# The two mixers of the second block reordered: gate work in PSUM, a projection chunk and the glu product between the levels

## The reference, cut to what matters

```python
u, q, k, v, g_out, a_low = jnp.split(h @ w_in[layer], IN_SPLITS, axis=-1)
y_s5 = _s5_group(u, ...)      # complex linear recurrence over time, 32 groups of 64 states, then
                              # gelu(y), and y * sigmoid(y @ w_glu + b_glu)
y_gla = _gla_group(q, k, v, g_out, a_low, ...)
y = jnp.concatenate([y_s5, y_gla], axis=-1) @ w_out[layer]

# in _gla_group: b = cumsum of log_sigmoid(a_low @ w_alpha_up + b_alpha) / 16 over time;
# scores[i, j] = sum over channels of q[i] * k[j] * exp(b[i] - b[j]) for j <= i, else 0;
# o = scores @ v, normalized, times silu(g_out)
```

## Time and profile before

| | us |
|---|---|
| median of 3 runs (2665.13 to 2666.99) | 2666.32 |
| the profiled execution's own time | 2666.25 |
| its span, first to last instruction | 2664.0 |
| mixer of l = 2, from the first transposes to the end of its output product | 836.5 to 1008.2 |
| mixer of l = 3, likewise | 1281.8 to 1444.2 |

### The profile page before, as it was taken

How to read it: one execution, slowest core, us unless ns; L and a number is a source line. 1 busy time by engine, 2 the same in 40 slices (tenths; PEclk the granted TensorE clock), 3 DMA queues, 4 the chain that set the end, 5 groups by cost and what they waited for, 6 DMA issues and landing times. The chain is left out here.

```text
span 2664.0 us, 37526 instructions
## 1 busy us (share of the span) xinstructions
PE 2506.8 (94%) x14758; PEld 2056.7 (77%) x14758; DVE 1810.9 (68%) x2036; ACT 1309.1 (49%) x1336; POOL 681.6 (26%) x359
## 2 busy tenths in 40 slices
PE   6999999998999988999887799999999999999996
PEld 4876898976998757899665688878787878888884
DVE  1664775665866757755674677777777787777785
ACT  2344543444442123333021666767776767667772
POOL 0000000005900717800451123323232323323322
PEclk9999999999999988999897899999999999999997
DMA  9996854586864556955331599999999999999992
GB/s 337 291 324 217 262 198 131 174 277 200 267 208 149 190 190 206 281 194 163 107 111 66 214 367 331 366 328 350 347 347 349 348 346 344 352 337 358 329 366 96
DMA packets 434956, 693.86 MB, mean 260 GB/s; under 512 B 37690, under 2 KB 255894, under 8 KB 434838
## 3 DMA queue, kind: packets, MB, share of 16 engines
q1 hardware_dynamic: 407632, 677.17, 73.8%
q10 hardware_dynamic: 27206, 15.03, 2.1%
HBM read 691.10 MB, written 1.05 MB: 260 GB/s over the span
## 5 line engine op out<-in xcount | busy, mean ns | idle before, releaser
L1430 ACT ACTIVATE region_part<-ring 128x2048 fp32r<-128x2048 f32 x448 | 835.4, 1907 | 275.0 <-PE bank L840 190.8
L840 PE MATMUL bank<-ring_part,region_part 128*128 128x512 f32 x1648 | 649.1, 394 | 0.0
L2306 DVE TENSOR_TENSOR ring_part<-ring,region_part 128x2048 fp32r<-128x2048 f32 x270 | 640.3, 2404 | 2.5 <-ACT region_part L1430 2.5
L838 PE MATMUL bank<-region_part 128*128 128x512 f32 x1432 | 582.6, 407 | 6.2 <-DVE ring_part L2306 6.2
L839 PE MATMUL bank<-region_part 128*128 128x512 f32 x1296 | 512.1, 395 | 0.0
L1320 POOL TENSOR_TENSOR ring_part<-ring,region_part 128x2048 fp32r<-128x2048 f32 x54 | 268.6, 4982 | 554.6 <-ACT region_part L1430 554.6
L840 PEld LDWEIGHTS bank<-ring_part,region_part 128*128 128x128 f32 x1648 | 309.8, 188 | 71.4
L838 PE MATMUL bank<-xn_part,region_part 128*128 128x256 f32 x1152 | 327.1, 284 | 10.4 <-DVE hT_part L2009 9.1
L838 PEld LDWEIGHTS bank<-region_part 128*128 128x128 f32 x1432 | 269.7, 188 | 75.6 <-issue 14.6
L840 PE MATMUL bank<-hT_part,region_part 128*128 128x256 f32 x1152 | 325.2, 282 | 0.0
L839 PE MATMUL bank<-xn_part,ring_part 128*128 128x256 f32 x1152 | 325.0, 282 | 0.0
(11 more groups left out here) (309 smaller groups left out, 4014.9 us busy)
## 6 DMA issues: line engine op xcount, KB each, us to landing
ring<-in_moe_w_gate SPq DMA_DIRECT2D x126, 1024.0 KB, 5.1
ring<-in_moe_w_up SPq DMA_DIRECT2D x126, 1024.0 KB, 5.2
ring<-in_moe_w_down SPq DMA_DIRECT2D x126, 1024.0 KB, 4.9
ring<-in_w_ada SPq DMA_DIRECT2D x48, 1024.0 KB, 7.7
ring<-in_mod_w SPq DMA_DIRECT2D x48, 1024.0 KB, 6.1
ring<-in_w_in SPq DMA_DIRECT2D x44, 1024.0 KB, 5.7
ring<-in_w_up_act SPq DMA_DIRECT2D x22, 1024.0 KB, 5.5
ring<-in_w_up_lin SPq DMA_DIRECT2D x22, 1024.0 KB, 5.7
```

The costliest lines, as they stand in the source:

```text
L838: nc.tensor.matmul(o, split(a_hi), split(b_hi), start=start, stop=False, skip_group_check=True)
L840: return nc.tensor.matmul(o, split(a_hi), split(b_lo), start=False, stop=stop, skip_group_check=True)
L1430: return nc.scalar.activation(out_, in_, func, **kw).then_inc(*done(*event))
L2306: v.tensor_tensor(split(w), w, whole(hi), ALU.subtract).then_inc(*done("moe_lo", j, e))
```

## The change

- PE order: `S5_CHUNKS` is now the flat order 8, 1, 2, 3, 6, 7, 4. The first pair of units is followed by chunks 8 and 1, the second by chunk 2, `s5_out(0, 1)` and the whole of chunk 3; then come `s5_in(4, 5)`, chunk 6, `s5_out(2, 3)`, `s5_in(6, 7)`, chunk 7, `s5_out(4, 5)`, chunk 4, `s5_out(6, 7)`. The modulation chunks are spread anew (`S5_ADA`).
- The glu product, in halves, follows levels 64 and 32; modulation chunks 12 and 13 follow level 16; the two token halves of chunk 5 follow levels 8 and 4 (`between`). The load order follows.
- DVE turns unit 3 back as well as unit 7, and scans and turns both in PSUM. `c_parts` is ahead of unit 0, `gate_start` after unit 1, `gate_sums` after unit 3 with its combine and running sums in bank 7; the division by 16 becomes the scale of ACT's exponentials. `y_sum(0)` follows unit 5, `y_sum(1)` follows the products for `off`.
- `gD`, `gQ`, `gK` and `scO` lie over table rows of units 0 to 3, `scT` over `ffn_rows`. The zeroing of `gQ` and `gK` is gone, that of `scT` is ahead of POOL's first unit. `gla` waits for POOL's unit 2 in place of the zeroing.
- Levels 64, 32 and 16 are copied into `scT` by ACT, block by block (2, 4 and 8 copies), not by DVE's mask. ACT does `gelu(1)` and the copies of `off` after the second exponential, and the chunk 5 copy after the last. The levels use four banks.

```diff
-DVE_UNITS = (7,)
-S5_CHUNKS = [(8, 1), (2, 3), (4, 5), (6, 7)]
+DVE_UNITS = (3, 7)
+S5_CHUNKS = (8, 1, 2, 3, 6, 7, 4)
+S5_ADA = {8: (0,), 1: (1,), 2: (2, 3), 3: (4,), 6: (5,), 7: (6, 7), 4: (8, 9, 10, 11)}
+GLA_CHUNK = 5
+BLOCKED = 3
...
+            plan.append((("in", l, GLA_CHUNK), ("pe_tile", "in", l, GLA_CHUNK)))
...
+    gD = ec[:, 0:1024].rearrange("p (b n) -> p b n", b=2)
+    gQ = ec[:, 1024:2048].rearrange("p (b n) -> p b n", b=2)
+    gK = es[:, 0:1024].rearrange("p (b n) -> p b n", b=2)
+    scO = es[:, 1024:1536].rearrange("p (b c i) -> p b c i", b=2, c=2)
+    scT = ffn_rows[:, 0:1024].rearrange("p (b j c i) -> p b j c i", b=2, j=2, c=2)
...
+                    o = bank(("lg", l), ("gla_z", l, 1), (7,))
...
+                    outs = [[bank(("bu", l, u, r), s5_rotated(l, u) if u in DVE_UNITS else ("s5_g", l, u), (2 * (u % 2) + r,)) for r in range(2)] for u in pair]
...
+                s5_in(0, 1)
+                projection(8)
+                projection(1)
+                alpha_low()
+                s5_in(2, 3)
+                projection(2)
+                s5_out(0, 1)
+                projection(3)
+                pe.wait_ge(*until("in_out", l, 1))
+                s5_in(4, 5)
+                projection(6)
+                s5_out(2, 3)
+                s5_in(6, 7)
+                projection(7)
+                s5_out(4, 5)
+                projection(4)
                 s5_out(6, 7)
-                key = ("glu", l)
-                pe.wait_ge(*loaded(key))
-                pe.wait_ge(*until("s5_gelu", l, 1))
...
+                def glu(b):
+                    key = ("glu", l)
+                    pe.wait_ge(*loaded(key))
+                    pe.wait_ge(*until("s5_gelu", l, 1))
+                    w = chunk(key)
                     o = bank(("glu", l, b), ("s5_sig", l, b), (b,))
...
+                def late_tokens(t):
+                    key = ("in", l, GLA_CHUNK)
...
+                    if t == 0:
+                        late[0] = bank(key, ("in_out", l, GLA_CHUNK), (4,)).rearrange("p (t n) -> p t n", t=NT)
+                    for k in range(KD):
+                        m = nc.tensor.matmul(late[0][:, t, :], hT[:, k, t * P:(t + 1) * P], w[:, k, :], start=k == 0, stop=k == KD - 1)
+                    if t:
+                        m.then_inc(*done("pe_tile", *key))
+                def between(n):
+                    if n < 2:
+                        glu(n)
+                    if n == 2 and l == 2:
+                        for q in range(12, ADA_MIX):
+                            ada_sum(3, "mix", q, 0)
+                    if n in (3, 4):
+                        late_tokens(n - 3)
+                usable[0] = (2, 3, 6, 7)
...
+                o = [bank(("off", l, par), ("gla_blocks", l, "off", par)) for par in range(2)]
...
+                    o = [bank(("lv", l, n, par), ("gla_blocks" if n < BLOCKED else "lv_out", l, n, par)) for par in range(2)]
...
-                pe.wait_ge(*until("off_out", l, 1))
+                    between(n)
+                pe.wait_ge(*until("gla_blocks", l, "off", 1))
+                pe.wait_ge(*until("gla_blocks", l, BLOCKED - 1, 1))
...
+                    pool.wait_ge(*until("pe_used", "down", l - 1, 0, ffn_groups(l - 1) - 1))
+                    nc.gpsimd.memset(scT, 0.0).then_inc(*done("gla_zero", l))
                     for u in range(8):
                         if u not in DVE_UNITS:
                             rotate(l, u)
-                    pool.wait_ge(*until("s5_y", l, 1))
-                    nc.gpsimd.memset(scT, 0.0).then_inc(*done("gla_zero", l, 0))
-                    nc.gpsimd.memset(gQ, 0.0).then_inc(*done("gla_zero", l, 1))
-                    nc.gpsimd.memset(gK, 0.0).then_inc(*done("gla_zero", l, 2))
...
-                for n in (0, 8, 1, 2, 3):
...
+                for n in (0, 8, 1, 2):
+                    features_out(n)
                 act.wait_ge(*until("gla_abs", l))
                 run(gz[:, 1], gz[:, 1], ACT.Exp, "act_chain", l, "lse")
                 act.wait_ge(*done.prev())
                 run(gz[:, 1], gz[:, 1], ACT.Ln, "gla_ln", l, bias=1.0)
-                for n in (4, 5, 6, 7):
+                features_out(3)
...
+                def gelu(qq):
                     act.wait_ge(*until("s5_y", l, qq))
                     v = uT[:, 2 * qq:2 * qq + 2, :].rearrange("p c s -> p (c s)")
                     run(v, v, ACT.Gelu_apprx_tanh, "s5_gelu", l, qq)
+                def blocks(n):
+                    h = LEVELS[n]
+                    for par in range(2):
+                        p_ = tile("lv", l, n, par).rearrange("p (a i) -> p a i", a=4)
+                        o = scT[:, par].rearrange("p j c i -> p (j c) i")
+                        for r in range(0, P, 2 * h):
+                            last = r + 2 * h == P
+                            run(o[r:r + h, :, r + h:r + 2 * h], p_[r:r + h, :, r + h:r + 2 * h], ACT.Copy,
+                                *(("gla_blocks", l, n, par) if last else ("act_chain", l, "block", n, par, r)))
+                for n in (6, 7):
+                    token_out(n)
+                gelu(0)
+                token_out(4)
+                load_rows(l, "mix")
+                act.wait_ge(*until("gla_zero", l))
                 for m, half in enumerate([P] + LEVELS[:-1]):
                     act.wait_ge(*until("gla_d", l, half))
-                    run(gD[:, m % 2, :], gD[:, m % 2, :], ACT.Exp, "gla_e", l, half)
-                    if m == 0:
+                    run(gD[:, m % 2, :], gD[:, m % 2, :], ACT.Exp, "gla_e", l, half, scale=1.0 / 16)
+                    if m == 1:
+                        gelu(1)
                         for par in range(2):
                             p_ = tile("off", l, par)
-                            run(scO[:, par].rearrange("p c i -> p (c i)"), p_[:, 0:S], ACT.Copy, "off_out", l, par)
+                            run(scO[:, par].rearrange("p c i -> p (c i)"), p_[:, 0:S], ACT.Copy, "gla_blocks", l, "off", par)
+                    if 2 <= m < 2 + BLOCKED:
+                        blocks(m - 2)
+                    if m == len(LEVELS) - 1:
...
+                    z = psum[bank_of["lg", l]]
                     dve.wait_ge(*until("gla_ln", l))
-                    v.scalar_tensor_tensor(gz[:, 0], gb, 0.0, gz[:, 1], ALU.min, ALU.subtract).then_inc(*link())
-                    after()
-                    v.tensor_scalar(gz[:, 0], gz[:, 0], 1.0 / 16, None, ALU.mult).then_inc(*link())
+                    after()
+                    v.scalar_tensor_tensor(z, gb.rearrange("p c s -> p (c s)"), 0.0, gz[:, 1].rearrange("p c s -> p (c s)"), ALU.min, ALU.subtract).then_inc(*link())
                     after()
                     for c in range(2):
-                        v.tensor_tensor_scan(gb[:, c, :], ones[:, 0:1].broadcast_to([P, S]), gz[:, 0, c, :], 0.0, ALU.mult, ALU.add)\
-                            .then_inc(*link())
+                        v.tensor_tensor_scan(gb[:, c, :], ones[:, 0:1].broadcast_to([P, S]), z[:, c * S:(c + 1) * S], 0.0, ALU.mult, ALU.add)\
+                            .then_inc(*(done("gla_z", l, 1) if c else link()))
...
+                c_parts()
                 dve.wait_ge(*until("tables", l))
                 after()
...
+                    if u >= 2 and u not in DVE_UNITS:
                         dve.wait_ge(*until(*s5_rotated(l, u - 2)))
                     for r, w in ((0, im), (1, re)):
...
+                            v.tensor_tensor_scan(w[:, jj, :] if u in DVE_UNITS else g5[:, u % 2, r, jj, :], s5p[:, l - 2, 0, j:j + 1].broadcast_to([P, S]),
...
+                        h = h5[:, u % 2]
                         dve.wait_ge(*until("pe_tile", "s5o", l, u - 2))
-                        v.tensor_tensor(h[:, 0], c, gg[:, 0], ALU.mult).then_inc(*link())
-                        v.tensor_tensor(w5[:, 0], s, gg[:, 1], ALU.mult).then_inc(*link())
-                        v.tensor_tensor(h[:, 1], s, gg[:, 0], ALU.mult).then_inc(*link())
-                        v.tensor_tensor(w5[:, 1], c, gg[:, 1], ALU.mult).then_inc(*link())
+                        v.tensor_tensor(h[:, 0], c, im, ALU.mult).then_inc(*link())
+                        v.tensor_tensor(h[:, 1], s, im, ALU.mult).then_inc(*link())
                         after()
-                        v.tensor_tensor(h[:, 0], h[:, 0], w5[:, 0], ALU.subtract).then_inc(*link())
-                        v.tensor_tensor(h[:, 1], h[:, 1], w5[:, 1], ALU.add).then_inc(*done(*s5_rotated(l, u)))
-                    after()
-                    if u == 0:
-                        c_parts()
-                    if u == 2:
+                        v.tensor_tensor(im, s, re, ALU.mult).then_inc(*link())
+                        v.tensor_tensor(re, c, re, ALU.mult).then_inc(*link())
+                        after()
+                        v.tensor_tensor(h[:, 0], h[:, 0], im, ALU.subtract).then_inc(*link())
```

(36 more changed lines are left out.)

78 lines of the change are left out of this document (26 added, 52 removed).

## The result

The changed kernel takes **2637.39 us** (median of 4 runs, 2635.92 to 2644.56), the kernel before 2665.73 in the same sitting (4 runs, 2664.5 to 2666.99): a ratio of 0.9899 with an interval of 0.9885 to 0.9913. That is 28.3 us faster. The forecast was 2645, with 2635 to 2656 as its range: the sign and the mechanism were right, and the time came out 7.6 us lower.

The account below looks back on a forecast made before the run. TensorE, busy 94%, was taken as the bound, with time only in its waits, mostly for VectorE. Savings of 11.7 (l = 2) and 13.4 us (l = 3), 25.1, less 4 for clock falls, took 2666.25 to 2645, range 2635 to 2656.

Parts of the forecast that it names:

- The wait at the fourth pair: Before the fourth pair's `s5_in`, TensorE was to wait for VectorE: 3.2 us in l = 2, 4.2 in l = 3.
- the sum: Units and levels added up over both mixers: 11.7 us saved in l = 2, 13.4 in l = 3, 25.1 in all.
- the fourth pair's charge: After the fourth pair's wait the clock falls: `s5_in` priced at 3.7 us, the projection behind it at 9.4.
- 20.8 and 11.8: TensorE's work in us before the third pair and before the fourth pair in l = 2.
- a gate at 4.65: Upper bound for the gate's combine and sums before unit 4, taken at 2.4 us; l = 3 would lose 2.5 more.
- rival A: In both mixers the clock never falls; 2.9 us more in l = 2, 1.8 in l = 3; 2636.5 us, chance 0.15.
- a separate charge: One more clock fall per layer around `off`, between 0 and 4.1 us, taken as 2, 4 for both layers.
- the four stretches: First pair to `off`, and `off` to `go`, in l = 2 and l = 3: forecast 216.4 us without the 4 us.
- The block copies: ScalarE's copies in the levels, 2, 4 and 8 a layer: between nothing and 0.60 us, taken as 0.26 each.
- rival B: ScalarE bounds the early levels, copies at 0.60 us and the gate at its upper bound; 2652 us, chance 0.11.
- under half of it: ScalarE's two extra table loads: the trace's 1.28 us each was set against the skill's 2.7 and used.
- Rivals C and D: C: TensorE stays at 1.2 GHz in levels, 2689 us, 0.04. D: experts or dense part absorb the gain, 2666, 0.04.

Follow-up runs that it names:

- the second execution: Second profiled execution of the unaltered changed kernel, taken when it was timed again with the experiments: span 2637.8 us; that measurement's median was 2637.98 us.
- the first execution: Profiled execution of the changed kernel's first measurement, slowest of its four runs: 2644.56 us, span 2642.7 us.
- the fill: Changed kernel plus matmuls whose results nobody reads, in TensorE's wait ahead of the fourth pair: long version 2637.66 us, short version 2638.09 us.

## Why the prediction was right, and where it was off

**Units.** The prices carried. The pairs were forecast at 15.5, 36.3 and 51.3 us behind the first in l = 2 (867.7, 888.5, 903.5) and came at 15.1, 35.8 and 50.8; in l = 3 at 15.0, 34.0 and 49.0 and came at 15.0, 34.6 and 49.6. The wait at the fourth pair was forecast at 3.2 and 4.2 and is 3.16 and 4.04. `off` in l = 3 was forecast at 75.8 and came at 75.7 in the second execution. In l = 2 it came 3.5 us earlier than the 81.0 of the sum. 0.5 of it is the pairs; 2.4 is the fourth pair's charge of 3.7 and 9.4 at 1.2 GHz (1.9 and 8.8 from start to start in the second execution, 3.2 and 9.1 in the first); the rest is the modulation chunks behind it and a slip of 0.2 in the sum, whose terms give 933.0. Its other slips are as small (20.7 and 11.7 for 20.8 and 11.8; 2.3 for the 2.5 of a gate at 4.65), and rival A's 2.9 and 1.8 are given without a working. The times that the prediction names for l = 3 are on the clock of the kernel before, so they have to be read from the first pair, as here.

**Levels.** 30.6 and 28.9 were forecast, 32.4 and 29.2 came, and in both layers 1.6 of it is the fall of the clock at level 64, which the sum held as a separate charge: level 64 and half of glu take 2.05 and 4.45 us in l = 2 of the second execution for 1.16 and 3.72, and 1.20 and 5.33 in l = 3. So by themselves the levels were 30.7 in l = 2, as forecast, and 27.5 in l = 3, 1.4 less. In the runs with the fourth unit on GpSimd, with the gate in SBUF and with `c_parts` put back the two groups of l = 2 took the shorter times and `go` came 1.6 us earlier, but then the products of `go` were slow instead, and the output product came only 0.7 earlier (36.0 us behind `off` for 36.7).

**The charges for the clock.** I set 2 us a layer, 4 in all, for one more fall of the clock around `off`, and charged the fourth pair's fall in full besides. The first came true in kind and nearly in size: 1.6 us a layer in both profiles. The second was too high in l = 2: 4.1 us for what took 1.7 in the second execution and 3.3 in the first. With the 4 us the forecast of the four stretches is 220.4 where the second execution has 214.7; of these 5.7 us, 3.5 are the units of l = 2, 1.7 the levels of l = 3 with their charge, and 0.5 the rest. That execution took 2639.64 us, and the other 2 us or so to the medians are what executions differ by. Without the 4 us the sum gives 2641, and rival A, with no fall at all, 2636.5, 1 us from the median. That is luck: the clock does fall, at the fourth pair, at level 64 and at the second pair of l = 3.

These runs show the fall paid where TensorE is the bound behind it. Behind the second pair it is (3.1 and 2.3 us more of the third pair's delay than the 4 of the wait). Behind the fourth it is only for what lies past GpSimd's unit 5, which `s5_out(4, 5)` needs and which ends some 63 us behind the first pair in l = 2 and 61 in l = 3, whether the fill is there or not: the output starts at 63.3 and 62.0 in the second execution, and at 64.8 in both layers in the first, where 1.7 of the 64.8 in l = 3 come from the second pair.

**The first execution is close to the forecast by luck.** It took 2644.56 us, but not for the forecast's reasons. Its l = 3 has a second pair of 2.82 and a chunk of 9.68 behind a wait of 1.27, the third pair at 36.3 for 34.6 and `off` at 78.5, where the forecast had that pair at full speed and `off` at 75.8; the units of l = 2 and the levels of l = 3 were shorter than forecast and make up for it. By their clocks the other three executions had fewer slow groups.

**Parts costed at nothing or near it.** `c_parts` ahead of unit 0 was free, as said, and undoing it costs 13.1 us: it is the largest single part. The gate's end was taken at 2.4 us of VectorE and was 1.41 and 1.26, 2.7. The reason given for it, that the sums read PSUM, does not hold: in SBUF they take 1.27. Its place in PSUM is worth nothing, both for that and since it stands in VectorE's slack ahead of the third pair's product (one wait at the fourth pair grew from 4.04 to 4.55 without it). The block copies were taken at 0.26 each and are 0.65 for 2, 1.14 for 4 and 1.89 for 8, starts included, so rival B's 0.60 had no footing; but undoing them costs nothing either, which the sum had not seen. The Trainium skill's 2.7 us for a table load (ScalarE: Activation LUTs, Table sets: the hidden batching unit) would have made it an estimated 5 us less gain. The changed trace has five such loads between 915 and 958 us, each of 1.28, and where the next activation waits for nothing else it starts within 0.02 us. By the Trainium skill (ScalarE: Activation LUTs, What ACT_TABLE_LOAD costs) the 2.7 is a load of about 1.28 us, which these rows match, and a drain of about 1.38, which no row here shows. So "under half of it" set a load beside a load with its drain, and by the price of both the sum would have been further off.

**Rivals C and D** are out: the levels ran at 0.95 and 0.94, and the experts' stretch took the saving over unchanged.

**What stays open.** The parts undone one at a time give back 13.1 (`c_parts`) and 7.6 (glu, chunk 5 and the two modulation chunks together, of which chunk 5 alone is worth -3.4), out of 27.6 to 28.3. The rest, some 7 us, I take to lie in the order of units and chunks, the zeroing moved ahead of the units and the waits these took away: 2.89 at the first factors, and 4.22 at the last output of l = 3 in the trace of before, below, where the second execution of the change waits 1.09. No run shows it.

```profile
1374.71 3.44 PE L974 MATMUL bank<-region 128*32 128x256 f32 x16 [4.22 <-DVE region L2556]
```

That order was not put back alone, and parts undone one by one need not add up.

## What to carry to other kernels

In these runs a stall that let the clock fall cost its own length plus the slow work behind it where the stalled engine was still the bound, and little where another engine was; look for which engine ends the next wait before you price it. When work is moved to fill gaps elsewhere, count what the place it left was hiding: here a chunk of 7.1 us left a wait of 3.2 to 4.0 behind, and half a chunk in each place was worth 6 to 7 us more. And undo each part by itself: of the five parts of this change that were undone, three, each plausible from busy times, earned nothing. Look at the rows of such a run too: an operation that was slow in the trace of before can be fast in its new place whatever memory it uses.

## What the runs showed of the hardware that I had not expected

The same wait is followed by different clocks. After 3.16 us of idle time `s5_in` took 3.31 us in one execution and 2.00 in another, with the chunk behind it at 9.19 and 8.86; the granted clock over the pair was 0.59 and 1.00, and over the first 4.6 and 4.0 us of the chunk 0.54 and 0.57:

```profile
902.20:905.40 3.20, 3.16 (x16) 2.53 (x16) 0.75 (x2) 0.00 (x0) 3.12 (x3) 0.59 0.56 180
905.40:910.00 4.60, 4.60 (x14) 3.67 (x13) 4.36 (x7) 0.00 (x0) 4.52 (x5) 0.54 0.00 0
```

```profile
902.60:904.50 1.90, 1.90 (x16) 1.59 (x16) 0.71 (x2) 0.00 (x0) 1.90 (x2) 1.00 0.94 295
904.53:908.50 3.97, 3.97 (x13) 3.20 (x12) 3.79 (x6) 0.00 (x0) 3.81 (x5) 0.57 0.00 0
```

And the wait of 1.27 us at the second pair of l = 3 was followed by a slow chunk in both profiles of the change (9.68 and 8.59), so the harmless wait of 2.05 in the earlier trace rows showed less than I had read into it. Such groups are what the two profiled executions differ in: of the 4.9 us between their spans 4.4 lie in the four stretches of the table, though all waits in them have the same length to within 0.02 us.

What made the gate's sums fast was their place in time, not PSUM. They fell from 3.25 us to 1.26 read from PSUM, but take 1.27 read from SBUF too (the run with the gate in SBUF). In l = 2 of the trace of before GpSimd works from 912.53 on, beside the sums at 912.76; in the changed kernel and in that run it is idle while they run (from 886.92 and from 884.55 on). So in these traces the length went with GpSimd's work beside them. The combination, which reads two operands from SBUF, gains nothing by writing to PSUM: 1.41 and 1.73 us in the first execution, 1.49 and 0.70 in the second, 1.37 and 0.72 with all of it in SBUF. What sets 0.7 or 1.4 there was not tested.
